# Recurrent mixer on six feature tiles of 128: padded gate blocks in one weight slot, queries ahead of the gates

## The reference

```python
z = x @ rglru_w_in                      # gate 768 | xr 768 | attention queries 256
xr = causal_conv(xr, conv_w, 4 taps) + conv_b
xb = xr.reshape(B, S, 8, 96)
r = sigmoid(einsum('bsgi,gij->bsgj', xb, w_a) + b_a)
i = sigmoid(einsum('bsgi,gij->bsgj', xb, w_x) + b_x)
log_a = -8 * r * softplus(-lam)
a, u = exp(log_a), sqrt(-expm1(2 * log_a)) * (i * xr)
h = scan(h = a * h + u) over the tokens
y = h * gelu(gate)
mix = concat([y, cross_attention(queries, mem)]) @ w_out
x = layer_norm(alpha * x + mix)
```

## Time and profile before

| | us |
|---|---|
| Median of 3 runs | 2787.41 (2785.59 to 2795.76) |
| The profiled execution | 2785.82 |
| Its span | 2784.1 |
| PE busy | 2462.1 (88%) |
| DVE busy | 1641.9 (59%) |
| POOL busy | 1112.0 (40%) |
| ACT busy | 896.6 (32%) |

### The profile page before, as it was taken

How to read it: one execution, slowest core, us unless ns; L and a number is a source line. 1 busy time by engine, 2 the same in 40 slices (tenths; PEclk the granted TensorE clock), 3 DMA queues, 4 the chain that set the end, 5 groups by cost and what they waited for, 6 DMA issues and landing times.

```text
span 2784.1 us, 26762 instructions
## 1 busy us (share of the span) xinstructions
PE 2462.1 (88%) x9068; PEld 1576.3 (57%) x9068; DVE 1641.9 (59%) x3322; ACT 896.6 (32%) x1766; POOL 1112.0 (40%) x1239
## 2 busy tenths in 40 slices
PE   8998978777779988887777778999899999999999
PEld 6864533322324744443332324888887878887787
DVE  1257657677663557656667765555665555547553
ACT  1122221221221421221221213445755444446543
POOL 0016666777774026766777773002700000025000
PEclk9999999999999999999999999999899999999999
DMA  7359999999997459999999996556035555542553
GB/s 232 121 177 394 401 395 406 409 409 403 409 409 291 136 189 399 399 406 404 409 409 405 410 409 260 174 200 174 16 128 167 197 184 179 188 150 77 182 181 121
DMA packets 322199, 766.68 MB, mean 275 GB/s; under 512 B 22064, under 2 KB 172496, under 8 KB 322064
## 3 DMA queue, kind: packets, MB, share of 16 engines
q0 software_dynamic: 150208, 546.77, 49.8%
q1 hardware_dynamic: 170576, 217.69, 24.0%
q10 hardware_dynamic: 1280, 0.50, 0.1%
HBM read 763.83 MB, written 1.05 MB: 275 GB/s over the span
## 4 chain that ended last, share of the span: by engine, by line
PE 48%; DMA 21%; DVE 15%; POOL 8%; issue 5%; ACT 3%; ACTq 0%; DVEq 0%; POOLq 0%
PE ps L293 29%; PE acc L293 17%; DMA arena<-in_peer_u,arena 17%; POOL arena L1298 7%; DMA arena<-in_peer_v,arena 4%; DVE arena L1244 4%; DVE arena L1173 1%; DVE arena L1179 1%; DVE arena L1175 1%; DVE arena L1177 1%; DVE arena L1171 1%; PE ps L1643 1%; ACT hi_ring L315 1%; DVE arena L1207 1%; DVE arena L1211 0%
## 5 line engine op out<-in xcount | busy, mean ns | idle before, releaser
L293 PE MATMUL acc<-arena 128*128 128x512 f32 (+2 forms) x2206 | 1030.8, 611 | 251.2 <-DMA arena<-in_peer_v,arena 145.7
L293 PEld LDWEIGHTS acc<-arena 128*128 128x128 f32 x2206 | 412.8, 200 | 848.4 <-issue 667.4
L1298 POOL DMA_INDIRECT arena<-in_peer_u,arena x512 | 484.5, 946 | 366.7 <-DVE arena L1217 172.4
L1298 POOL DMA_INDIRECT arena<-in_peer_v,arena x512 | 486.1, 949 | 200.1 <-issue 129.9
L1244 DVE CUSTOM_DVE_ANT_0 arena<-arena,ps 128x1024 f32<-128x1024 f32 x256 | 306.6, 1219 | 223.2 <-DMA arena<-in_peer_u,arena 220.4
L1244 DVE CUSTOM_DVE_ANT_0 arena<-arena,acc 128x1024 f32<-128x1024 f32 x256 | 305.9, 1219 | 198.4 <-DMA arena<-in_peer_u,arena 196.7
L323 DVE TENSOR_TENSOR lo_ring<-ring,hi_ring 128x2048 fp32r<-128x2048 f32 x136 | 310.2, 2290 | 166.9 <-ACT hi_ring L315 163.6
L293 PE MATMUL ps<-x_fm,ring 128*128 128x256 f32 (+4 forms) x1792 | 354.3, 360 | 9.1 <-DMA ring<-in_peer_w_q 3.4
L293 PEld LDWEIGHTS ps<-x_fm,ring 128*128 128x128 f32 (+2 forms) x1792 | 304.2, 189 | 64.3 <-issue 11.9
L293 PE MATMUL ps<-hi_ring,x_hi 128*128 128x512 f32 x704 | 284.9, 405 | 11.8 <-DVE k_mem L1752 6.8
L315 ACT CAST hi_ring<-ring 128x2048 fp32r<-128x2048 f32 x136 | 258.1, 1911 | 70.9 <-DMA ring<-in_ffn_w 70.9
(11 more groups left out here) (383 smaller groups left out, 2307.7 us busy)
## 6 DMA issues: line engine op xcount, KB each, us to landing
ring<-in_ffn_w SPq DMA_DIRECT2D x132, 1024.0 KB, 5.5
ring<-in_peer_w_q SPq DMA_DIRECT2D x16, 1024.0 KB, 6.0
ring<-in_mlstm_w_in SPq DMA_DIRECT2D x12, 1024.0 KB, 5.2
arena<-in_peer_u,arena POOLq DMA_INDIRECT x512, 11.2
arena<-in_peer_v,arena POOLq DMA_INDIRECT x512, 11.4
ring<-in_cv_w_in SPq DMA_DIRECT2D x8, 1024.0 KB, 5.8
ring<-in_rglru_w_in SPq DMA_DIRECT2D x8, 768.0 KB, 21.9
ring<-in_w_out SPq DMA_DIRECT2D x5, 1024.0 KB, 5.0
```

The costliest lines, as they stand in the source:

```text
L293: return pe.matmul(o, l, r, start=first, stop=last)
L1298: pool.indirect_dma_start(ring_[:, g % slots, :], None, table, bass.IndirectOffsetOnAxis(ix[j % 4][:, k:k + 1].bitcast(U32), 0), element_o ...
```

## The change

The 768 features now lie in 6 tiles of 128. The chunks are three `r.x` and three `r.g` of 256 columns; `w_out` has 6 + 2 feature tiles. A gate matrix of 96 x 96 now lies across tile borders, so for each output tile there is a 128 x 128 block of its own tile and a piece with 64 rows of a neighbour. All pieces of both gates go as `r.ai` into one ring slot (4 x 448 columns) and, for the corners, into a spare part of `mix_fm`. What lies between the pieces must be zero: DVE clears the slot and the corners in round 8 of peer0, and SP waits for that before it fetches the pieces with 20 small loads. PE does the queries before the gates, and ACT reads them before the Sigmoids. PE waits for the pieces on a semaphore of their own. The parameter columns move to 6 rows of 128 for each parameter.

```diff
-    for c in range(4):
-        columns(f"r.x{c}", w, RG_B * RG_D + 192 * c, 192)
-    plan.append(("r.a", A["rglru_w_a"][0].rearrange("g i j -> i g j"), RG_D, RG_B, RG_D))
-    plan.append(("r.i", A["rglru_w_x"][0].rearrange("g i j -> i g j"), RG_D, RG_B, RG_D))
-    columns("r.q", w, 2 * RG_B * RG_D, 256)
-    for c in range(4):
-        columns(f"r.g{c}", w, 192 * c, 192)
-    mix_out(1, RG_D, RG_B)
+    for c in range(3):
+        columns(f"r.x{c}", w, RG_W + 256 * c, 256)
+    plan.append(("r.ai", None, P, 4, 448))
+    columns("r.q", w, 2 * RG_W, 256)
+    for c in range(3):
+        columns(f"r.g{c}", w, 256 * c, 256)
+    mix_out(1, P, RG_K)
...
+GATE_PIECES = ((0, 0, 96, 0, 96, 0, 0), (1, 0, 32, 0, 32, 96, 96), (1, 0, 32, 32, 96, 96, 384), (1, 32, 96, 32, 96, 0, 128),
+               (2, 0, 64, 0, 64, 64, 192), (2, 64, 96, 0, 64, 0, 384), (2, 64, 96, 64, 96, 0, 256), (3, 0, 96, 0, 96, 32, 288))
+GATE_CORNERS = ((1, 32, 96, 0, 32, 0, 96), (2, 0, 64, 64, 96, 64, 0))
...
+                if name == "r.ai":
+
+                    nc.sync.wait_ge(dve_steps, count_of("gate blocks cleared"))
+                    for gate, w in enumerate((A["rglru_w_a"][0], A["rglru_w_x"][0])):
+                        blocks = ring[:, slot, 896 * gate:896 * gate + 896].rearrange("p (a c) -> p a c", a=2)
+                        for pair, pieces in ((blocks, GATE_PIECES), (gate_corners[:, 2 * gate:2 * gate + 2, :], GATE_CORNERS)):
+                            for b, r0, r1, c0, c1, row_at, col_at in pieces:
+                                nc.sync.dma_start(pair[row_at:row_at + r1 - r0, :, col_at:col_at + c1 - c0],
+                                                  w[b::4, r0:r1, c0:c1].rearrange("g i j -> i g j")).then_inc(
+                                    sems["gate_blocks"], landed("gate_blocks", "gate blocks loaded"))
+                    continue
...
+                if i == 0 and j == PR_HEADS:
+                    dve.wait_ge(pe_steps, count_of("used " + ring_at["r.ai"][2]))
+                    dve.memset(ring[:, ring_at["r.ai"][0], 0:4 * 448], 0.0).then_inc(dve_steps, VE.step())
+                    dve.memset(gate_corners, 0.0).then_inc(dve_steps, VE.step("gate blocks cleared"))
...
+            w = chunk("r.q", TE)
+            pe_columns("r.xq", w, x_fm)
+            release("r.q")
+            pe.wait_ge(sems["gate_blocks"], count_of("gate blocks loaded"))
+            for m in range(RG_K):
+                pe_gate_tile(m)
+            release("r.ai")
...
+        def pe_gate_tile(m):
+
+            half, k = m // 3, m % 3
+            for b in range(3 * half, 3 * half + (2, 3, 3)[k]):
+                pe.wait_ge(dve_steps, count_of(f"xc {b}"))
+            blocks = ring[:, ring_at["r.ai"][0], 0:4 * 448].rearrange("p (g c) -> p g c", g=4)
+            o = open_tile(f"r.g{m}.ri")
+            low, high = slice(0, 64), slice(64, P)
+            for gate in range(2):
+                g, out_ = 2 * gate + half, o[:, S * gate:S * gate + S]
+                own, x_own = blocks[:, g, P * k:P * k + P], xc[:, m, :]
+                if k == 1:
+                    mm(out_[low, :], blocks[high, g, 384:448], xc[high, m - 1, :], True, False)
+                    mm(out_[high, :], blocks[low, g, 384:448], xc[low, m + 1, :], True, False)
+                    i = mm(out_, own, x_own, False, True)
+                else:
+                    part, x_next = (low, xc[low, m + 1, :]) if k == 0 else (high, xc[high, m - 1, :])
+                    mm(out_, own, x_own, True, False)
+                    i = mm(out_, gate_corners[part, g, :], x_next, False, True)
+            i.then_inc(pe_steps, TE.step(f"tile r.g{m}.ri"))
```

More of the change, by code:

```diff
@@ L33 @@
 RG_B, RG_D = 8, 96
+RG_W = RG_B * RG_D
+RG_K = RG_W // P
 RG_CONV = 4
@@ L151, in slots_of @@
         n = at % slots
-        fills[n] = fills.get(n, 0) + 1
+        fills[n] = fills.get(n, 0) + (name != "r.ai")
         place[name] = (n, fills[n], last.get(n))
@@ L176 @@
 COL_ROWS = 104
-RG_CB, RG_BA, RG_BX, RG_LAM = 32, 40, 48, 56
+RG_CB, RG_BA, RG_BX, RG_LAM = (RG_K * (RG_CONV + n) for n in range(4))
 def build(nc, A, out, known):
@@ L690, in dve_setup @@
             dve.tensor_copy(col_s5[:, 0:96], o[:, 352:448]).then_inc(dve_steps, VE.step())
-            dve.tensor_copy(col_rg[:, :], o[0:RG_D, 448:512]).then_inc(dve_steps, VE.step("read par"))
+            dve.tensor_copy(col_rg[:, :], o[:, 448:496]).then_inc(dve_steps, VE.step("read par"))
             o = tile_of(VE, "sd")
@@ L712, in pe_params @@
             pe.transpose(o[:, 352:448], st_s[0:96, :], ident[0:96, 0:96])
-            pe.transpose(o[0:RG_D, 448:512], st_r[0:64, :], ident[0:64, 0:64]).then_inc(pe_steps, TE.step("tile par"))
+            pe.transpose(o[:, 448:496], st_r[0:48, :], ident[0:48, 0:48]).then_inc(pe_steps, TE.step("tile par"))
             o = open_tile("sd")
@@ L1325, in pool_peer @@
                         gather(v // PR_K, v % PR_K, v_ring, "v_rows", V_SLOTS, "v", v_table)
-        x_pad = area(0, RG_B, S + RG_CONV - 1)
-        xc, r_g, i_g, a_t, th, l1, gg = (area(2072 + 2048 * n, RG_B, S) for n in range(7))
+        x_pad = area(0, RG_K, S + RG_CONV - 1)
+        xc, r_g, i_g, a_t, th, l1, gg = (area(1600 + 1536 * n, RG_K, S) for n in range(7))
         xq1, p1, pT1 = area(16408, 2, S), area(16920, XA_HEADS, TT, S), area(18968, XA_HEADS, 2, S)
-        sp_c = area(21016, 4, RG_B)
+        sp_c = area(21016, 4, RG_K)
+        gate_corners = mix_fm[:, KD:KD + 2, :].rearrange("p a (b c) -> p (a b) c", c=P)
         def pe_rglru():
-            for c in range(4):
+            for c in range(3):
                 w = chunk(f"r.x{c}", TE)
                 if c == 0:
-                    pe_token_halves("xrt", "r.x0", lambda half: w[:, :, half * RG_D:half * RG_D + RG_D], RG_D)
+                    pe_token_halves("xrt", "r.x0", lambda half: w[:, :, half * P:half * P + P])
                 else:
-                    pe_columns(f"r.x{c}", w, x_fm, RG_D)
+                    pe_columns(f"r.x{c}", w, x_fm)
                 release(f"r.x{c}")
[L1342 to L1349, removed]
             w = chunk("r.q", TE)
@@ L1352, in pe_rglru @@
             release("r.q")
-            for c in range(4):
+            pe.wait_ge(sems["gate_blocks"], count_of("gate blocks loaded"))
+            for m in range(RG_K):
+                pe_gate_tile(m)
+            release("r.ai")
+            for c in range(3):
                 w = chunk(f"r.g{c}", TE)
-                pe_columns(f"r.gate{c}", w, x_fm, RG_D)
+                pe_columns(f"r.gate{c}", w, x_fm)
                 release(f"r.g{c}")
-            pe_attention(1, xq1, lambda h: p1[:, h, :, :], lambda h: pT1[:, h, :, :], RG_B)
+            pe_attention(1, xq1, lambda h: p1[:, h, :, :], lambda h: pT1[:, h, :, :], RG_K)
             pe.wait_ge(act_steps, count_of("xa1 ready"))
@@ L1371, in act_rglru @@
             act.activation(sp_c[R, 1, :], sp_c[R, 1, :], ACT.Ln, bias=1.0).then_inc(act_steps, AC.step("log1p lam"))
-            for b in range(RG_B):
+            o = tile_of(AC, "r.xq")
+            act.copy(xq1.rearrange("p a b -> p (a b)"), o).then_inc(act_steps, AC.step("read r.xq"))
+            found["xq1 ready"] = (AC.who, AC.n)
+            for b in range(RG_K):
                 o = tile_of(AC, f"r.g{b}.ri")
@@ L1387, in act_rglru @@
             act.activation(th[R, :, :], th[R, :, :], ACT.Sqrt, scale=2.0).then_inc(act_steps, AC.step("sqrt parts"))
[L1388 to L1391, removed]
+            for c in range(3):
                 o = tile_of(AC, f"r.gate{c}")
                 act.activation(gg[R, 2 * c:2 * c + 2, :].rearrange("p a b -> p (a b)"), o[R, :], ACT.Gelu).then_inc(act_steps, AC.step(f"read r.gate{c}"))
-            act_attention(1, lambda h: p1[:, h, :, :], lambda h: pT1[:, h, :, :], RG_B)
+            act_attention(1, lambda h: p1[:, h, :, :], lambda h: pT1[:, h, :, :], RG_K)
         def dve_rglru():
-            R = slice(0, RG_D)
-            lam = col_rg[:, RG_LAM:RG_LAM + RG_B]
+            R = slice(0, P)
+            lam = col_rg[:, RG_LAM:RG_LAM + RG_K]
             dve.tensor_scalar(sp_c[R, 0, :], lam, -1.0, None, ALU.mult).then_inc(dve_steps, VE.step())
@@ L1421, in dve_rglru @@
             dve.wait_ge(dve_steps, VE.n)
-            dve.wait_ge(act_steps, count_of(f"read r.g{RG_B - 1}.ri"))
+            dve.wait_ge(act_steps, count_of(f"read r.g{RG_K - 1}.ri"))
             dve.tensor_tensor(i_g[R, :, :], i_g[R, :, :], xc[R, :, :], ALU.mult).then_inc(dve_steps, VE.step())
@@ L1433, in dve_rglru @@
             attention_softmax(1, lambda h: p1[:, h, :, :], None, 0)
[L1434 removed]
+            for c in range(3):
                 dve.wait_ge(act_steps, count_of(f"read r.gate{c}"))
[L1436 removed]
+            dve.tensor_tensor(mix_fm[R, 0:RG_K, :], r_g[R, :, :], gg[R, :, :], ALU.mult).then_inc(dve_steps, VE.step("y rglru"))
             dve_mix_ln(1, 0)
```

25 lines of the change are left out of this document (12 added, 13 removed).

## The result

| | before | changed kernel |
|---|---|---|
| Median of 16 runs each, us | 2790.37 (2785.59 to 2795.76) | 2794.76 (2790.2 to 2802.52) |
| The profiled execution, us | 2785.82 | 2802.52 |
| Its span, us | 2784.1 | 2800.8 |

The ratio is 1.0018, with a 95% interval of 1.001 to 1.0025: 4.4 us slower by the medians, where 4.7 us faster was forecast. It lies within the 0.5% that I named, but above the range of 2775 to 2790.

A forecast was written before the change was run, and what follows sets the result against it. Full DMA engines bound the gather stages peer0 and peer1, a PE-DVE chain of waits the mixer. Terms -6.2 + 0.9 - 3.5 - 0.2 + 5.8 + 0 + 0 - 1.5 = -4.7 us on 2787.4 gave 2783, range 2775 to 2790.

The forecast's parts named there:

- Part 1: PE's columns in the mixer: fewer groups, gates in 14.6 us; a gain of 6.2 us, bounds 4.5 to 10.4.
- rival B: Gate matmuls on PE: changing the number of rows costs nothing, 4.2 us more gained, 2778.5 us; chance 0.10.
- rival D: Gate matmuls on PE: pairs of 64-row pieces run one after the other, sharing one bank, 2784.4 us; chance 0.18.
- part 2: Mixer, queries ahead of the gates: PE does not wait for DVE's taps; nothing lost.
- part 3: Mixer, DVE: the recurrence's chain becomes visible, a new delay of 0.9 us; bounds 0 to 2.
- part 4: Output product: eight feature tiles instead of ten, 3.5 us gained in token half 0, 0.2 more in half 1.
- Part 5: Loads in peer0: about two more megabytes in the full DMA stage, a loss of 5.8 us; bounds 0 to 7.
- Rival A: Loads in peer0: they are hidden, 5.8 us less, 2777 us; chance 0.15.
- Rival C: Loads in peer0: narrow runs in a full queue make it slower, 2801 us at 148 ns a packet; chance 0.09.
- Part 6: DVE clearing the slot in round 8 of peer0: 2.0 us, covered by waits, so 0; worst case 2.0.
- Part 7: Loads in peer1: one megabyte fewer there, a gain of 1.5 us; at most 3.0, at least 0.

The follow-up runs named there:

- e1: The changed kernel run again, nothing edited: 2797.45 us, 1.0036 to the kernel before.
- e3: The changed kernel with col_rg 64 columns wide again, so the arena stands at its old address: 2785.58 us, 0.999 to the kernel before.
- e6: The kernel of e3 with hi_ring alone 64 bytes lower, at its address in the changed kernel: 2792.17 us, 1.001 to the kernel before.
- e5: The kernel of e3 with the loads of r.q and r.g0 also waiting until r.x0 is used: 2780.95 us, 0.9963 to the kernel before.
- e2: The kernel before run again, nothing edited: 2790.98 us, 1.0011 to the kernel before.
- e9: The kernel of e5 with col_rg 80 columns wide and hi_ring 64 bytes lower within the arena: 2744.47 us, 0.984 to the kernel before.
- e7: The changed kernel (col_rg 48 columns wide) with hi_ring alone 64 bytes lower: 2782.84 us, 0.9971 to the kernel before.
- e10: The kernel of e3 with the gathered rows' rings, and scores and queries behind them, 64 bytes higher: 2749.79 us, 0.9853 to the kernel before.

## Why the prediction was wrong

**The step that failed is the sum.** It added up seven parts and took everything behind peer1 as unchanged. The narrower `col_rg` was an edit with a term of its own, and it had none, not even as a bound: +11.2 us by the trace (4 x 2.8), 11.9 by e1 against e3. So the range ended too low and no rival covered the case. By e6, `hi_ring` accounts for 1.7 of each 2.8; which other tile brings the rest stays open. The base had a share in the miss of the range, not in that of the direction: I put the sum on a median of three runs, 2787.4, and that of 16 is 3.0 us higher. e3, which is the changed kernel without this term, has 0.999; -4.7 us would have been 0.9983, inside its interval.

**Part 1 held.** PE's timeline of the changed mixer, from the first gate matmul to the scores:

```profile
932.51 0.59 PE L299 MATMUL ps<-arena,ring 128*128 128x256 f32 x2
933.04 0.70 PE L299 MATMUL ps<-arena,mix_fm 64*128 64x256 f32 x2
...
934.92 2.92 PE L299 MATMUL ps<-arena,ring 64*64 64x256 f32 x14
937.77 0.70 PE L299 MATMUL ps<-arena,mix_fm 64*128 64x256 f32 x2
...
946.89 20.99 PE L299 MATMUL ps<-x_fm,ring 128*128 128x256 f32 x96
967.81 2.10 PE L299 MATMUL ps<-k_mem,arena 64*128 64x256 f32 x16
```

The gates take 946.89 - 932.51 = 14.38 us; 14.6 was forecast. An alternating matmul takes 0.62 to 0.63, which is 0.433 + 0.19 (933.04 to 933.66, 934.29 to 934.92): rival B falls. Tile 1 and the matmul behind it are seven (14 records) in 937.77 - 934.92 = 2.85 us. With four changes and no overlap they would take 7 x 0.433 + 4 x 0.19 = 3.8, with two pairs side by side 2.9: rival D falls. The profile has the first records of both pieces of a pair in the same 0.43 us:

```profile
934.92 0.43 PE L299 MATMUL ps<-arena,ring 64*64 64x256 f32 x2
```

The rule of the Trainium skill (TensorEngine Tiling (Array Packing), Restrictions and Gotchas) by which row tiles cannot share a PSUM bank at the same time would have given 3.8; the trace (2.85) doesn't agree for these two pieces, which go to one bank but to different halves of its partitions.

**Parts 2 to 4 held.** The chain in the changed mixer:

```profile
906.16 62.85 PE ps L299 x288
969.05 0.68 DVE arena L1469
969.75 0.70 DVE stat L465
...
980.61 14.02 PE acc L299 x32
```

PE runs through queries and gates without a gap (part 2), DVE's first maximum follows directly behind the scans (part 3), and the product of half 0 takes 14.02, 14 was forecast (part 4). From the first `r.x` to the product it is 980.61 - 906.16 = 74.45 against 79.65 before: -5.2, the forecast was -6.2 + 0.9 = -5.3. From there to the index table it is 37.25 against 40.70: -3.45, the forecast -3.7. Between LayerNorm and `r.x0` this execution lost 0.8.

**Part 5 held.** +5.5 us in peer0, and e5 takes it back; forecast 5.8. The round behind the clearing is the longer one, as forecast, but by 8.1 us instead of 6: 50.0 (560.44 to 610.43) against 41.9 for the same round before:

```profile
562.49 0.17 DVE L1217 SCALAR_TENSOR_TENSOR arena<-arena 128x16 uint32<-128x16 f32 x1
...
604.38 0.17 DVE L1217 SCALAR_TENSOR_TENSOR arena<-arena 128x16 uint32<-128x16 f32 x1
```

The five rounds ahead of it are 2.6 us shorter together; the gate matrices were loaded there before. Rival A falls. Rival C falls too: with the narrow pieces in peer0, e5 has 620.0 us there against 620.25 before. (Where the prediction speaks of rows of 512 KB, a gather has 512 KB; a row has 4.)

**Part 6 held.** DVE's timeline of round 8: the clearing takes 2.0 us, the dot product behind it does not wait, and the next already waits 0.36.

```profile
540.55 1.55 DVE L1290 MEMSET ring<- 128x1792 f32 x1 [0.32 <-issue]
542.16 0.48 DVE L1291 MEMSET mix_fm<- 128x512 f32 x1
542.56 1.16 DVE L1261 CUSTOM_DVE_ANT_0 arena<-arena,ps 128x1024 f32<-128x1024 f32 x1
...
544.09 1.22 DVE L1261 CUSTOM_DVE_ANT_0 arena<-arena,ps 128x1024 f32<-128x1024 f32 x1 [0.36 <-DMA arena<-in_peer_u,arena]
```

**Part 7 was mis-sized:** 0 instead of -1.5, 620.26 against 619.91 in peer1. The query chunk that went out at 1019.96 now goes out at 1014.72, ahead of peer1, yet the first round is as long as before (30.8 us against 30.9). What paces it was not tried; that it is POOL was only argued.

Without the missing term these values add up to -5.2 - 3.45 + 5.5 + 0.35 = -2.8 us, the 0.999 of e3; with its 11.2 they give +8.4. The medians show +4.4 in the first 16 runs and +7.8 in e1. What makes the two sets differ stays open; by e2, a difference of this size lies near what the ratios can tell.

## What to carry to other kernels

A change to the size of a small tile moves every tile behind it. List which tiles move, and by what remainder, before calling the rest of the program unchanged; allocate what PE streams and what gathers write first, at addresses that no later edit shifts. And when untouched code changes its pace while busy share and clock stay the same, compare counts in equal windows and move one tile at a time.

## What the hardware showed beyond that

- In the up products, two of three matmuls of 512 columns stream from `hi_ring`. With `hi_ring` 64 bytes off a multiple of 128 they come some 2% slower as a whole: 336 or 337 instead of 343 in 75 us. The down products follow no such simple rule: a matmul of `hi_ring` and `a_hi` takes 396 ns in e3, 400 in e1 and e9, 393 in e6 and 392 in e7. What combination of addresses counts there was not tried.
- In the full gather stage, 417 or 418 GB/s come in when the rows of 4 KB are written to the one multiple of 256 bytes that was tried, and 406 at 64, 128 or 192 bytes behind one. In both stages together this is some 36 us (e3 against e10). The Trainium skill's page DMA: Bandwidth & Descriptors, section How a descriptor splits into AXI transactions, says that a transaction must start at a multiple of 256 bytes, and that a descriptor that starts elsewhere fetches bytes ahead of its start that it doesn't use and that cost beats; it speaks of reading, and the place moved here is the one written to. The traces are in keeping with a border of 256 there too, but show no extra that grows with the distance: 406 GB/s at all three.
